# Router logits of a fused transformer kernel: token tiles held still in TensorE, narrow router weights streamed, first tile's products between the two tiles' transposes

## The reference, cut to what matters

```
# first block, both layers (l = 0, 1)
scores = softmax(xt @ w_router + b_router)            # xt: 256 x 1024, w_router: 1024 x 16
# best of 4 groups by the sum of its top two, the top two inside it, renormalised
# second block
g_logits = hf @ w_rg + b_rg                            # 1024 x 4
e_logits = hf @ w_re + b_re                            # 1024 x 16
```

## Time and profile before

| | |
|---|---|
| median of 3 runs | 1635.25 us (1633.97 to 1637.89) |
| the profiled execution: its own time | 1635.94 us |
| its span, first to last instruction | 1634.2 us, so 1.7 us lie around it |
| mean granted TensorE clock | 0.974 of full |
| PE, PEld, DVE, ACT, POOL busy | 94%, 79%, 78%, 68%, 4% of the span |

### The profile page before, as it was taken

One profiled execution on the slowest core, in us unless ns is written; L12 is line 12 of the kernel. 1 busy time (PEld: TensorE's weight loads), 2 busy tenths in 40 slices (PEclk: granted clock), 3 DMA queues, 4 the chain that ended last, 5 costly groups with the idle time before them and its releaser, 6 DMA issues.

```text
span 1634.2 us, 21033 instructions
## 1 busy us (share of the span) xinstructions
PE 1531.4 (94%) x8087; PEld 1289.4 (79%) x8087; DVE 1273.8 (78%) x1594; ACT 1119.2 (68%) x1340; POOL 57.2 (4%) x94
## 2 busy tenths in 40 slices
PE   7999989999997999998999998898999899999976
PEld 5789867888886788976888886787887678888855
DVE  4667468999997486457999998558656789999964
ACT  4444438999994544446999997266454489999952
POOL 5000010000001000000000000000000000000000
PEclk9999999999998999999999999999999999999988
DMA  9356328999996545625999999343434479999950
GB/s 326 127 202 206 129 103 316 394 392 392 392 396 247 174 155 178 209 103 191 382 388 393 392 395 341 119 155 103 155 129 142 148 285 382 393 390 394 394 207 26
DMA packets 176693, 422.75 MB, mean 259 GB/s; under 512 B 7052, under 2 KB 7216, under 8 KB 176576
## 3 DMA queue, kind: packets, MB, share of 16 engines
q1 hardware_dynamic: 172400, 407.92, 68.3%
q0 software_dynamic: 4176, 13.30, 2.5%
HBM read 420.15 MB, written 1.05 MB: 258 GB/s over the span
## 4 chain that ended last, share of the span: by engine, by line
PE 71%; DVE 17%; ACT 6%; issue 3%; DMA 2%; POOL 1%; POOLq 0%; ACTq 0%; DVEq 0%
PE ps L975 14%; DVE w_low L1666 11%; PE ps L1001 7%; PE ps L687 5%; PE ps L688 4%; PE ps L692 4%; PE ps L1012 4%; PE ps L735 3%; PE ps L984 3%; PE ps L797 3%; ACT w_high L1351 3%; PE ps L736 3%; PE ps L804 3%; PE ps L798 3%; PE ps L740 3%
## 5 line engine op out<-in xcount | busy, mean ns | idle before, releaser
L1666 DVE TENSOR_TENSOR w_low<-raw,w_high 128x1024 fp32r<-128x1024 f32 x588 | 694.6, 1225 | 229.8 <-ACT w_high L1351 226.7
L1351 ACT ACTIVATE w_high<-raw 128x1024 fp32r<-128x1024 f32 x588 | 598.3, 1056 | 314.5 <-PE ps L692 119.4
L1001 PE MATMUL ps<-w_high,hT 128*128 128x512 f32 x384 | 153.5, 400 | 0.3
L975 PE MATMUL ps<-w_high,x_first 128*128 128x512 f32 x384 | 153.3, 399 | 0.4 <-ACT x_first L1404 0.3
L1001 PE MATMUL ps<-w_low,hT 128*128 128x512 f32 x384 | 152.8, 398 | 0.0
L975 PE MATMUL ps<-w_low,x_first 128*128 128x512 f32 x384 | 151.1, 394 | 0.0
L687 PE MATMUL ps<-w_high,act_high 128*128 128x512 f32 x272 | 111.1, 409 | 6.4 <-DVE w_low L1666 3.6
L1666 DVE TENSOR_TENSOR w_low<-work,w_high 128x1024 fp32r<-128x1024 f32 x96 | 113.4, 1227 | 0.0
L688 PE MATMUL ps<-w_low,act_high 128*128 128x512 f32 x272 | 109.4, 402 | 0.0
L1666 DVE TENSOR_TENSOR w_low<-x_res,w_high 128x1024 fp32r<-128x1024 f32 x90 | 106.3, 1227 | 0.0
L692 PE MATMUL ps<-w_high,act_low 128*128 128x512 f32 x272 | 104.6, 398 | 0.0
(11 more groups left out here) (372 smaller groups left out, 3079.9 us busy)
## 6 DMA issues: line engine op xcount, KB each, us to landing
raw<-in_w_up SPq DMA_DIRECT2D x96, 1024.0 KB, 9.0
raw<-in_w_gate SPq DMA_DIRECT2D x51, 1024.0 KB, 9.2
raw<-in_w_down SPq DMA_DIRECT2D x48, 1024.0 KB, 8.9
work<-in_w_gate SPq DMA_DIRECT2D x45, 1024.0 KB, 9.0
x_res<-in_w_down SPq DMA_DIRECT2D x45, 1024.0 KB, 8.5
raw<-in_w_in SPq DMA_DIRECT2D x44, 1024.0 KB, 5.9
raw<-in_w_out SPq DMA_DIRECT2D x12, 1024.0 KB, 4.9
raw<-in_wk_x SPq DMA_DIRECT2D x8, 1024.0 KB, 5.4
```

Of the source, the lines that this page charges most:

```text
L975: i = pe.matmul(HS[:, part, :], own_rows(e, 2 * j + c), weights(u, 512 * c, 512 * c + 512)[half_w], start=(j + c + half_w == 0), stop=(j + ...
L1001: i = pe.matmul(YS[:, b, :], hT[:, k, :], weights(u, 512 * b, 512 * b + 512)[half_w], start=(k + half_w == 0), stop=(k + half_w == FC))
L1351: A(split_unit(n)[0], raw_unit(n), ACT.Copy).then_inc(high_ready, 1)
L1666: V.tensor_tensor(split_unit(n)[1], raw_unit(n), split_unit(n)[0].bitcast(F32), ALU.subtract).then_inc(low_ready, 1)
```

## The change

The logits are computed in the other orientation. The stationary operand is a 128x128 block of the token tile (`act_high` or `act_low`), and the 16 or 20 router columns are streamed, so the result lies in PSUM with tokens on partitions, each tile in a bank of its own. ACT's copy `narrow_copied`, the two small transposes and the slot of `routerT` go. `routed_tiles` puts the high products of tile 0 (16 matmuls) between tile 0's transposes and tile 1's idle matmuls; after tile 1's transposes come its 16 high products, tile 0's 8 low ones and tile 1's 8 low ones. The idle matmuls before tile 1 become 5 instead of 7, and 3 instead of 4.

```diff
-        plan_in(slots, L + turned_input + "0", L + turned_input + "1", L + "routerT", L + "router", L + "pos")
+        plan_in(slots, L + turned_input + "0", L + turned_input + "1", L + "router", L + "pos")
...
-        plan_routing(L, "x2T", (3, 2, 0, 1, 0))
+        plan_routing(L, "x2T", (3, 2, 0, 1))
...
-    plan_routing("2.", "x1T", (3, 0, 1, 0, 1))
+    plan_routing("2.", "x1T", (3, 0, 1, 0))
...
+            def logits(name, turned, c0, width):
+                nh, nl = nar_high[:, :, c0:c0 + width], nar_low[:, :, c0:c0 + width]
+                begin(name)
+                def with_high(t):
+                    high_made(turned[t])
+                    for c in range(KC):
+                        xh = act_high[:, c, t * P:t * P + P]
+                        pe.matmul(slot_banks(name)[:, t, 0:width], xh, nh[:, c, :], start=(c == 0), stop=False)
+                        pe.matmul(slot_banks(name)[:, t, 0:width], xh, nl[:, c, :], start=False, stop=False)
+                def with_low(t):
+                    wait_released(pe, turned[t])
+                    for c in range(KC):
+                        i = pe.matmul(slot_banks(name)[:, t, 0:width], act_low[:, c, t * P:t * P + P], nh[:, c, :], start=False, stop=(c == KC - 1))
+                    return i
+                with_high(0)
+                yield
+                with_high(1)
+                with_low(0)
+                full(with_low(1), name)
+                yield
+
+            def routed_tiles(src, L, turned, before, c0, width, idle):
+                steps = logits(L + "router", turned, c0, width)
+                for t in range(TT):
+                    turn_tiles(src[:, t:t + 1, :], turned[t:t + 1], S["normed"], before + t, idle=(idle[t],))
+                    next(steps)
...
-                turn_tiles(x, (L + "x2T0", L + "x2T1"), S["normed"], TT * (3 * l + 1), idle=(2, 7))
-                narrow(L + "router", N_R, NE, (L + "x2T0", L + "x2T1"))
+                routed_tiles(x, L, (L + "x2T0", L + "x2T1"), TT * (3 * l + 1), N_R, NE, (2, 5))
...
-            turn_tiles(h_tok, ("2.x1T0", "2.x1T1"), S["normed"], TT * (3 * DEPTH + 2), idle=(2, 4))
-            narrow("2.router", N_RE, NE + 4, ("2.x1T0", "2.x1T1"))
+            routed_tiles(h_tok, "2.", ("2.x1T0", "2.x1T1"), TT * (3 * DEPTH + 2), N_RE, NE + 4, (2, 3))
...
-                narrow_copied(L + "router", NE)
...
-            narrow_copied("2.router", NE + 4)
...
-                src = slot_ps(name)[:, 0:TT * NE].rearrange("p (t n) -> p t n", t=TT)
+                src = slot_banks(name)[:, :, 0:NE]
...
-                src = slot_ps(name)[:, 0:TT * (NE + 4)].rearrange("p (t n) -> p t n", t=TT)
+                src = slot_banks(name)[:, :, 0:NE + 4]
```

## The result

The kernel after takes 1649.44 us (median of 4 runs, 1647.79 to 1651.12) against 1635.85 us for the kernel before on the same chip: ratio 1.0092 [1.0073, 1.0110]. It is slower by 13.6 us by the difference of the medians and by 15 us by the ratio. On the median that the prediction stands against, 1635.25, the ratio gives 1650.3 us. Predicted were 1643.7 us and a range of 1635 to 1650. The sign is as forecast, and so in the main is the mechanism; the size is not: the span grew by 1648.5 - 1634.2 = 14.3 us instead of 8.5.

What follows compares the result with a forecast made beforehand. It took matmuls to bound the span and routing to be a single file; +1.3 us at full clock and +7.2 from clock falls made +8.5, 1643.7 us against a median before of 1635.25, range 1635 to 1650, forecast case 0.68.

Steps and rivals of the forecast that it cites:

- The spacing of the products, 0.11 us from the count's matmuls: Routing stage: the 48 new products start 0.11 us apart, set by loading 128-column blocks, as in the expert count.
- Both rivals with fast loads: Router products 0.07 us apart or less: about 1631 us without more falls (chance 0.12), 1636 with one per stage (0.06).
- Behind tile 1's copy at full clock, a gain of 0.07 us: From tile 1's first product to the logits: 3.71 us against 3.78, 0.07 gained per stage, 0.2 in all.
- Tile 1 late by 0.35, 0.35 and 0.80 us at full clock: Tile 1's transposes queue behind tile 0's 16 products and idle matmuls; with the 0.21 gain, +1.3 us at full clock.
- DVE's idle time before the logits: A sign that the forecast is right: DVE's idle time before it reads the logits grows; no size given.
- A fall in each narrow stretch: Two narrow stretches per routing stage, before and behind tile 1's transposes, each lower the clock; 5.5 falls in three stages.
- The rival that narrow products hold the clock up: No added clock falls in the routing stages: only +1.3 us, 1636.6, or 1635.0 if layer 0's fall goes; chance 0.14.
- I expect a fall in each: Routing stages: 5.5 falls at 1.59 us, 8.75, less the one already in layer 0: +7.2 us.
- The likeliest case's own range: From one fall fewer per stage (1638.9) to doubled first low stretches (+4.8, 1648.5) and one more gather fall (1650.1).
- The falls at the gather "as before": The clock fall at the gather behind the routing stage is taken as unchanged, adding nothing to the sum.

Runs made afterwards that it cites:

- e1_wide: The changed kernel with each product streaming its router columns 15 or 12 times over, 240 columns, copies unread; 1639.31 us, ratio 1.0023.
- e3_by_tile: The change's order of tiles alone, with the operands, ACT copy and small transposes of the kernel before; 1633.53 us, ratio 0.9990 to before.
- e7: The changed kernel with router columns streamed 4 or 3 times, 64 or 60 columns; 1649.07 us, ratio 1.0087.
- e9: The changed kernel with only tile 1's 24 products, high and low, streaming 240 columns; 1642.83 us, ratio 1.0044.
- e8: The changed kernel with only tile 0's 16 high products streaming 240 columns; 1643.76 us, ratio 1.0049.
- e2: The change's new orientation alone: all 48 products behind tile 1's transposes, idle matmuls as in the kernel before; 1649.78 us, ratio 1.0087.
- e10: Kernel before with the change's tile order, old operands, and unread wide matmuls in PE's waits, in the second block in a free slot; 1629.01 us, ratio 0.9962.
- e11: The kernel before, its order and operands untouched, with more unread wide matmuls in PE's waits; 1629.77 us, ratio 0.9980.
- e4_idle_ahead: The changed kernel with three idle matmuls before tile 1 moved ahead of tile 0's products, into PE's wait for ACT; 1646.63 us, ratio 1.0068.

## Why the prediction was off, point by point

- *The spacing of the products, 0.11 us from the count's matmuls:* right, 0.111 us. The fp32r loads of 128 columns take 190 to 192 ns at full clock. Both rivals with fast loads fell. The prediction took a gain for fp32r from the Trainium skill's rule of the fast weight load (TensorE: Matmul & The Clock Gate, section Weight-path perf modes), which asks for 128 weights and a type that isn't FP32. The same table says that this load reads 32 bits at a time and wins nothing for fp32, so it does not promise a gain for a type of four bytes. The rows show none; whether the fast load was on, no run here shows. (The kernel declares these blocks as `F32R`; the rows list them as f32.)
- *Behind tile 1's copy at full clock, a gain of 0.07 us:* right where it can be seen (0.15 us in layer 1).
- *Tile 1 late by 0.35, 0.35 and 0.80 us at full clock:* the mechanism is right (no wait before L844), and with the clock the delay was 2.12, 3.76 and 1.27 us, 7.15 together. Predicted with the clock: 1.5 + 2.5 x 1.59 = 5.5. DVE's idle time before the logits grew as forecast in layer 0 (3.12 to 3.79 us) and in the second block (1.52 to 1.97), not in layer 1 (1.53 to 1.44).
- *A fall in each narrow stretch:* right in number: six low stretches up to the residual's end, for 5.5 forecast. In part that is luck. In layer 1 the clock fell at 739.9 with one narrow product done, and e1_wide and e3_by_tile have a fall at the same place (733.1 and 733.5), where the products stream 240 and 128 columns. So that fall is not the work of the narrow products; their part is its length, 6.8 us for 3.4. The rival that narrow products hold the clock up fell: the change is at 0.50 from 235 to 245, and with 240 columns (e1_wide) the same place is at 1.00.
- **The step that failed** is the price in "I expect a fall in each": 1.59 us for each, "+7.2 us" in all, which against the span should have been about 13. The 1.59 was read from a fall in the kernel before, where the products stream 256 columns and the clock is back after 3.4 us (233.6 to 237.0). In the change half of the low stretches last longer: 10.2 us in layer 0 (234.7 to 244.9), 6.8 us in layer 1 (739.9 to 746.7) and 6.8 in the second block (1316.7 to 1323.5). The other three last 3.4 us each (227.9 to 231.3, 753.5 to 756.9, 1309.9 to 1313.3). At the price of 1.59 us for 3.4 us, all 34 us come to 15.9 us, an estimate, less before's 1.59 and with the 1.3 of full clock 15.6, against 14.3 measured: the price per microsecond was about right, the length was not.
- *What sets the length:* ahead of tile 1 in layer 1 it goes with the products: 6.8 us in the three runs where tile 0's stream 16 or 64 columns (the change, e7, e9), 3.4 us in those where they stream 128 or 240 (e3, e1, e8). Behind tile 1 the cause of the length stays open: in the second block the fall at 1316.7 is followed by 1.1 us of narrow products and then by the residual, and the clock still stays low for 6.8 us.
- *What the low stretches hit:* the long ones of layer 0 and of the second block, and in layer 1 the one from 753.5, slow the residual, which takes 5.38 to 6.53 us for 3.70, and the count L1096, the selection and the gather are queued behind it on PE. Predicted for all behind tile 1's start were 3 x 1.59 - 1.59 - 0.21 = 3.0 us; measured 1.5 + 5.35 = 6.85. The likeliest case's own range had a first low stretch of twice the length (+4.8 us); it lacked the same for the second.
- *The falls at the gather "as before":* right in number, two before (from 752.4 and 1312.2) and two after (from 248.3 and 1327.0), though not in the same layers.

The runs show that the clock is the cause of about 10 of the 14 us (e1_wide, 10.1), and that the new operands bring the loss about and the new order doesn't (e2 against e3). Why 64 columns at the same spacing count for no more than 16 is not settled.

## What to carry to other kernels

In these runs a product costs the longer of its load and its stream. At full clock, holding 128 columns made each one 0.11 us whatever it streamed (16, 64 or 240 columns), where holding 16 columns and streaming 128 made it 0.06 us. The Trainium skill gives a load the time of its columns over 1.2 GHz (TensorE: Matmul & The Clock Gate, section LDWEIGHTS); by that I estimate 107 ns for 128 columns. The spacing of 0.111 us at full clock agrees; the 190 ns that the rows list for one load do not, and at half clock the spacing was 0.21 us. And around runs of such narrow products the clock was low for 34 us in the three stages, whatever the busy share said. Don't take the price of a fall from a place where other work follows it: here low stretches lasted 3.4, 6.8 and 10.2 us. Count, too, what is queued behind. Unread wide matmuls in the waits, in a slot whose `begin` waits for nobody, kept the clock at 1.00 up to the gather in e10 and e11, whose products stream 128 and 256 columns. For the change's own narrow products only e4_idle_ahead tried some, and 2.8 us came back; filling all waits there was not tried.

## What the runs showed of the hardware that was not expected

- With TensorE listed busy for 10.00 of 10 us, 30 matmuls in them, the granted clock was 0.50 all along (235 to 245 of the change). In e7_four_times the same held with the weight loads listed busy for 4.00 of 4 us.
- Products 0.11 us apart at full clock gave the same time with 16 and with 64 streamed columns (1649.44 and 1649.07 us), and 1639.31 us with 240.
- More work took less time twice: 12 to 15 times the streamed columns (e1_wide, 10.1 us below the change), and 22 more unread matmuls in the kernel before (e11_fill_only, 0.9980 of its time).
